# Seven-product 2x2 block groups in the gate and up projections, with the first weight sums on GpSimd

## What is computed

```python
x = x + jnp.concatenate([mix, mem_out], axis=-1) @ w_o[i]
gate, up = _split(rms_norm(x, norm_ffn[i]) @ w_gate_up[i], (D_FF, D_FF))
x = x + (jax.nn.silu(gate) * up) @ w_down[i]
```

## Time and profile before

| | |
|---|---|
| median of 3 runs | 2190.85 us (2190.31 to 2191.6) |
| the profiled execution, whole | 2190.48 us |
| its span in the profile | 2188.8 us |
| busy: TensorE, DVE, ACT, GpSimd | 99%, 59%, 47%, 3% of the span |
| bytes read from HBM | 411 MB, 189 GB/s over the span |

### The profile page before, as it was taken

The page is one execution under the profiler, slowest core; times in us unless marked ns, Lnnn a source line. Parts: engine busy times, 40 slices in busy tenths (PEclk is TensorE's granted clock), DMA queues, the critical chain, the costliest instruction groups (busy, mean ns, idle before and its releaser), DMA issues.

```text
span 2188.8 us, 29206 instructions
## 1 busy us (share of the span) xinstructions
PE 2175.4 (99%) x10172; PEld 1811.1 (83%) x10172; DVE 1293.3 (59%) x1555; ACT 1029.5 (47%) x1310; POOL 58.7 (3%) x99
## 2 busy tenths in 40 slices
PE   8999999999999999999999999999999999999999
PEld 7888888888888888888888888888888888888887
DVE  6767766555555555555566767675555555554443
ACT  7755654444444444444444445454444444443332
POOL 2101100000000000000100000000000000000000
PEclk9999999999999999999999999999999999999999
DMA  8765476766676666666555656577666766666664
GB/s 311 239 194 154 135 214 208 212 202 202 204 211 204 204 198 198 209 204 202 178 173 163 198 166 190 163 221 221 202 202 205 210 204 204 200 213 203 202 203 133
DMA packets 244562, 435.48 MB, mean 199 GB/s; under 512 B 23040, under 2 KB 43648, under 8 KB 244480
## 3 DMA queue, kind: packets, MB, share of 16 engines
q1 hardware_dynamic: 243392, 432.31, 64.8%
q10 hardware_dynamic: 1088, 2.10, 0.2%
HBM read 411.25 MB, written 2.10 MB: 189 GB/s over the span
## 4 chain that ended last, share of the span: by engine, by line
PE 99%; ACT 0%; DVE 0%; DMA 0%; issue 0%; DVEq 0%; SPq 0%; ACTq 0%
PE unit_bank L1629 95%; PE mix_bank L1652 1%; PE mix_bank L1782 1%; PE mix_bank L1717 0%; PE mix_bank L1679 0%; PE mix_bank L1726 0%; PE mix_bank L1768 0%; DVE w_lo L1005 0%; DMA source_T<-in_mem_T 0%; PE mix_bank L1690 0%; PE mix_bank L1701 0%; PE mix_bank L1813 0%; PE mix_bank L1811 0%; PE mix_bank L1804 0%; PE mix_bank L1794 0%; ACT p_a L675 0%
## 5 line engine op out<-in xcount | busy, mean ns | idle before, releaser
L1005 DVE TENSOR_TENSOR w_lo<-raw,w_hi 128x1024 fp32r<-128x1024 f32 x767 | 932.2, 1223 | 757.9 <-ACT w_hi L582 738.1
L582 ACT ACTIVATE w_hi<-raw 128x1024 fp32r<-128x1024 f32 x767 | 808.9, 1060 | 904.8 <-PE unit_bank L1629 875.4
L1629 PE MATMUL unit_bank<-w_hi,hT_hi 128*128 128x512 f32 (+1 forms) x1984 | 615.0, 391 | 0.0
L1629 PE MATMUL unit_bank<-w_hi,hT_lo 128*128 128x512 f32 (+1 forms) x1984 | 610.2, 389 | 0.0
L1629 PE MATMUL unit_bank<-w_lo,hT_hi 128*128 128x512 f32 (+1 forms) x1984 | 609.8, 389 | 0.0
L1629 PEld LDWEIGHTS unit_bank<-w_hi,hT_lo 128*128 128x128 f32 x1984 | 372.3, 188 | 76.5
L1629 PEld LDWEIGHTS unit_bank<-w_lo,hT_hi 128*128 128x128 f32 x1984 | 372.3, 188 | 76.5
L1629 PEld LDWEIGHTS unit_bank<-w_hi,hT_hi 128*128 128x128 f32 x1984 | 368.8, 188 | 72.8 <-DVE w_lo L1005 0.2
L1629 PE MATMUL unit_bank<-w_hi,gT_hi 128*128 128x512 f32 x704 | 217.0, 389 | 0.0
L1629 PE MATMUL unit_bank<-w_lo,gT_hi 128*128 128x512 f32 x704 | 216.9, 389 | 0.0
L1629 PE MATMUL unit_bank<-w_hi,gT_lo 128*128 128x512 f32 x704 | 216.8, 389 | 0.0
(11 more groups left out here) (232 smaller groups left out, 1028.3 us busy)
## 6 DMA issues: line engine op xcount, KB each, us to landing
raw<-in_w_gate_up SPq DMA_DIRECT2D x352, 512.0 KB, 4.3
raw<-in_w_down SPq DMA_DIRECT2D x176, 512.0 KB, 4.5
raw<-in_w_in_b SPq DMA_DIRECT2D x104, 512.0 KB, 4.0
raw<-in_w_o SPq DMA_DIRECT2D x64, 512.0 KB, 4.4
raw<-in_w_in_a SPq DMA_DIRECT2D x40, 512.0 KB, 4.1
moved<-turned SPq DMA_DIRECT2D x528, 32.0 KB, 3.1
raw<-in_w_mem_kv SPq DMA_DIRECT2D x31, 512.0 KB, 5.6
tanh_ff<-act_ff SPq DMA_DIRECT2D x112, 32.0 KB, 3.3
```

The costliest lines, as they stand in the source:

```text
L582: act.activation(w_hi[:, s, :, :], raw[:, s, :, :], ACT.Copy).then_inc(sems["hi_ready"], 1)
L1005: dve.tensor_tensor(w_lo[:, s, :, :], raw[:, s, :, :], w_hi[:, s, :, :].bitcast(F32), ALU.subtract).then_inc(sems["lo_ready"], 1)
L1629: ins = pe.matmul(unit_bank[2 * pair + tile][:, 0:cols], stationary[part][:, kt + j, tile * P:(tile + 1) * P], b[:, s, j, 0:cols], start=o ...
```

## The change

In the ten looped chunks of both layers, gate and up run side by side. The pieces of a chunk alternate: gate and up columns for the same 256 rows. Such a pair of pieces is a 2 x 2 block of weights (two row blocks; gate and up), and with the two token tiles and two feature blocks of `hT` it is a 2 x 2 by 2 x 2 block product. For two of the eight pairs of a chunk (`SEVEN = (2, 5)`) it is made from seven block products in place of eight, 21 matmuls of 512 columns in place of 24. That needs sums of activation blocks, made once for each layer (`seven_forms`, and the second token block in `hT` is overwritten by its difference from the first), and four sums of weight blocks for each group: two at once on GpSimd (`first_sums`, 1024 columns), two on DVE. Each sum is split into hi and lo like a weight. Four of the seven products go into the chunk's other four banks ("shared"); these are combined behind the group's last pieces (`shared_products`) and added to the chunk's own banks at its end (`own_products`), after which silu and the product with up follow in the next chunk. The first chunk of a layer has no groups.

The weights' side of a group, on ACT, GpSimd and DVE, and TensorE's order:

```diff
+                                pool.wait_ge(sems["hi_ready"], t.value("hi_ready"))
+                                pool.wait_ge(sems["piece_used"], t.value("split", RING))
+                                pool.tensor_tensor(sums[:, :, :], blocks[:, 1:3, :], blocks[:, 0:1, :].broadcast_to([P, 2, COLS]),
+                                                   ALU.add).then_inc(sems["sum_ready"], 1)
...
+            def split_seven():
...
+                act.wait_ge(sems["piece_used"], t.value("split", RING))
+                act.activation(four_blocks(w_hi, s)[:, 1:4, :], four_blocks(raw, s)[:, 1:4, :],
+                               ACT.Copy).then_inc(sems["hi_ready"], 2)
+                act.wait_ge(sems["sum_ready"], t.next("sum_ready"))
+                act.activation(sums_hi[:, :, :], sums[:, :, :], ACT.Copy).then_inc(sems["sum_hi_ready"], 1)
+                act.wait_ge(sems["sum_ready"], t.next("sum_ready"))
+                act.activation(w_hi[:, s, 0, :], w_sum[:, s, 0, :], ACT.Copy).then_inc(sems["sum_hi_ready"], 1)
+                act.wait_ge(sems["lo_ready"], t.value("split"))
+                act.activation(sum_all_hi[:, :], sum_all[:, :], ACT.Copy).then_inc(sems["sum_hi_ready"], 1)
...
+            def split_seven():
...
+                dve.wait_ge(sems["hi_ready"], t.next("hi_ready", 2))
...
+                dve.tensor_tensor(low[:, 1:4, :], blocks[:, 1:4, :], high[:, 1:4, :].bitcast(F32),
+                                  ALU.subtract).then_inc(sems["raw_lo_ready"], 1)
+                dve.wait_ge(sems["sum_ready"], t.next("sum_ready"))
+                dve.tensor_tensor(w_sum[:, s, 0, :], sums[:, 1, :], blocks[:, 1, :], ALU.add).then_inc(sems["sum_ready"], 1)
+                dve.wait_ge(sems["sum_ready"], t.next("sum_ready"))
+                dve.tensor_tensor(sum_all[:, :], w_sum[:, s, 0, :], blocks[:, 3, :], ALU.add).then_inc(sems["lo_ready"], 2)
+                dve.wait_ge(sems["sum_hi_ready"], t.next("sum_hi_ready"))
+                dve.tensor_tensor(sums_lo[:, :, :], sums[:, :, :], sums_hi[:, :, :].bitcast(F32),
+                                  ALU.subtract).then_inc(sems["sum_lo_ready"], 1)
+                dve.wait_ge(sems["sum_hi_ready"], t.next("sum_hi_ready"))
+                dve.tensor_tensor(w_lo[:, s, 0, :], w_sum[:, s, 0, :], w_hi[:, s, 0, :].bitcast(F32),
+                                  ALU.subtract).then_inc(sems["sum_lo_ready"], 1)
+                dve.wait_ge(sems["sum_hi_ready"], t.next("sum_hi_ready"))
+                dve.tensor_tensor(sum_all_lo[:, :], sum_all[:, :], sum_all_hi[:, :].bitcast(F32),
+                                  ALU.subtract).then_inc(sems["sum_lo_ready"], 1)
...
+                pe.wait_ge(sems["raw_lo_ready"], t.next("raw_lo_ready"))
+                product(own[1], x12, w_hi[:, s + 1, 1, :], w_lo[:, s + 1, 1, :], False, False)
+                product(own[0], form[2], w_hi[:, s, 1, :], w_lo[:, s, 1, :], False, False)
+                if first:
+                    pe.wait_ge(sems["shared_free"], t.next("shared_free"))
+                product(shared[0], x11, w_hi[:, s + 1, 0, :], w_lo[:, s + 1, 0, :], first, last)
+                pe.wait_ge(sems["sum_lo_ready"], t.next("sum_lo_ready"))
+                product(shared[1], form[0], sums_hi[:, 1, :], sums_lo[:, 1, :], first, last)
+                product(shared[2], x21_less_x11, sums_hi[:, 0, :], sums_lo[:, 0, :], first, last)
+                pe.wait_ge(sems["sum_lo_ready"], t.next("sum_lo_ready"))
+                product(shared[3], form[1], w_hi[:, s, 0, :], w_lo[:, s, 0, :], first, last)
+                pe.wait_ge(sems["sum_lo_ready"], t.next("sum_lo_ready"))
+                product(own[3], x22, sum_all_hi[:, :], sum_all_lo[:, :], False, False).then_inc(sems["piece_used"], 2)
```

`product` is three matmuls into one bank. The order within a chunk, for position i of 16 (DVE; ACT has the same with `gate_tanh` at 1, a copy of `shared[0]` at 12 and `moved_block` at 14), and SP's:

```diff
+                    for i in chunk_pieces():
                         if i == 1:
+                            gate_silu()
+                        if i == 5:
+                            times_up()
+                        if i == 13:
+                            shared_products(shared)
+                        if i == 14:
+                            moved_block(gT, j * 4, "gT_ready")
+                    own_products(own)
...
+                chunk_turns = moves({11: (0, 6), 12: (6, 12), 13: (12, 16)})
```

More of the change, by code:

```diff
@@ L63 @@
 LEVELS = 7
+QUAD_PIECES = 2
+CHUNK_PIECES = KT
+SEVEN = (2, 5)
+SEVEN_APART = 6
 MASKED = -1e38
@@ L1014, in pieces, with chunk_pieces @@
                         split()
+                    t.move("at")
+            def split_seven():
+                s = slot[0] % RING
+                slot[0] += 2
+                dve.wait_ge(sems["hi_ready"], t.next("hi_ready", 2))
+                t.move("split", 2)
+                dve.wait_ge(sems["piece_used"], t.value("split", RING))
+                blocks, low, high = (four_blocks(ring, s) for ring in (raw, w_lo, w_hi))
+                dve.tensor_tensor(low[:, 1:4, :], blocks[:, 1:4, :], high[:, 1:4, :].bitcast(F32),
[13 more added lines that the diff above has]
+                                  ALU.subtract).then_inc(sems["sum_lo_ready"], 1)
+            def chunk_pieces():
+                for i in range(CHUNK_PIECES):
+                    yield i
+                    ahead = (i + LEAD) % CHUNK_PIECES
+                    if ahead // 2 not in SEVEN:
+                        split()
+                    elif ahead % 2 == 0:
+                        split_seven()
                     t.move("at")
@@ L1472, in times_up @@
[L1472 to L1480, removed]
-                        if i == 1:
-                            moved_block(gT, (j - 1) * 4, "gT_ready")
-                    times_up()
+                        ins = dve.scalar_tensor_tensor(out=up_ff[:, s, :], in0=up_ff[:, s, :],
+                                                       scalar=half_rs2[:, s:s + 1], in1=tanh_ff[:, s, :], op0=ALU.mult,
+                                                       op1=ALU.mult)
@@ new lines, in chunk_products @@
+            def chunk_products(own, shared):
+                pe.wait_ge(sems["own_free"], t.next("own_free"))
+                for q in range(CHUNK_PIECES // 2):
+                    if q in SEVEN:
+                        seven_products(SEVEN.index(q), own, shared)
+                        continue
+                    for n in range(2):
+                        s = slot[0] % RING
+                        slot[0] += 1
+                        pe.wait_ge(sems["lo_ready"], t.next("lo_ready"))
+                        for j in range(2):
+                            for m, (part, b) in enumerate(((0, w_hi), (1, w_hi), (0, w_lo))):
+                                for tile in range(TILES):
+                                    ins = pe.matmul(own[2 * tile + n][:, :], hT[part][:, 2 * q + j, tile * P:(tile + 1) * P],
+                                                    b[:, s, j, :], start=q == 0 and j == 0 and m == 0,
+                                                    stop=q == CHUNK_PIECES // 2 - 1 and j == 1 and m == 2)
+                        ins.then_inc(sems["piece_used"], 1)
@@ L1901, in projection_ffn @@
                     pass
-                parts = [unit(hT, p, kts, opens=n == 0, closes=n == 2) for n, kts in enumerate(FIRST_KTS) for p in (pair, other)]
+                parts = [unit(hT, p, kts, opens=n == 0, closes=n == 2) for n, kts in enumerate(FIRST_KTS) for p in (2, 3)]
+                settled(0, 1, 2, 3)
                 for i in products(*parts):
```

217 lines of the change are left out of this document (176 added, 41 removed).

## The result

The changed kernel takes 2211.86 us (median of 4 runs, 2211.76 to 2213.44) beside 2190.9 before: a ratio of 1.0098, 95% interval 1.0083 to 1.0113. 1% slower; forecast were 2208 us and slower with a chance of 0.78. The profiled execution took 2211.83 us, its span 2210.0, 21.2 us over that of before.

A forecast was written before the change was run, and what follows sets the result against it. TensorE's matmul count was taken as the bound: 2190.5 - 27.2 us for matmuls removed + 40 x 1.12 us of waits for GpSimd's held-up sum = 2208 us, range 2190 to 2233.

The forecast's parts named there:

- What bounds, and what is saved: TensorE's matmul count bounds the kernel; 40 groups with 3 matmuls fewer each take 27.2 us off if it never waits.
- GpSimd held up by DVE's instruction: In each group, GpSimd's sum waits for DVE's whole three-block subtraction and ends at 3.35 + T us.
- Rival 1: GpSimd's sum is not held up by DVE's subtraction, so all of the saving stays: 2163.3 us; chance 0.13.
- T = 2.38 us: Time of GpSimd's 1024-column sum by itself: 2.38 us, the middle of 1.95 and 2.82.
- Rival 2: GpSimd's sum takes two steps a column, T near 1.95 us; the wait eats the saving: 2190 us; chance 0.07.
- The wait, 1.12 us: TensorE waits T - 1.26 = 1.12 us for `sums_lo` at each group's tenth matmul, against 0.68 saved: +17.6 us.
- the prediction's zero: The moment at which TensorE begins the second piece ahead of a group; the group's steps are timed from it.
- Rival 3: Five hand-overs on the chain at 0.08 us, not 0.04: +8 us, with T = 2.82 2233 us; chance 0.05.
- Rival 4: GpSimd goes first and DVE's subtraction waits; `w_sum` 0.1 us sooner, same time within 4 us; chance 0.03.
- DVE's, ACT's and SP's queues at no cost: In a chunk, the added DVE work, ACT's copies and SP's later loads delay nothing; DVE has 35.8 of 44.4 us.
- A chunk of 44.4 us: A looped chunk was forecast to take 44.4 us, with TensorE idle about 1.1 us in each group.

The follow-up runs named there:

- experiment 1: Changed kernel with DVE's subtraction of the three low parts made to wait until GpSimd's sum is done: 2218.71 us, ratio 1.0128.
- experiment 4: Changed kernel with `sum_all` moved behind `sums_lo` in DVE's queue, nothing else changed: 2236.57 us, ratio 1.0208.
- experiments 1 and 2: The second: changed kernel with DVE's subtraction of 1536 columns split into three instructions of 512: 2212.44 us, ratio 1.0099. The first: see experiment 1.
- experiment 3: Changed kernel with GpSimd's sum made twice in a row: 2380.33 us, ratio 1.0865; with only half the sum, 512 columns: 2177.83 us, ratio 0.9940.

## Why the prediction was right

- **What bounds, and what is saved.** Right. TensorE runs 120 matmuls fewer and is the bound wherever it doesn't wait; the kernel with DVE's sum first gets 20 of the 27.2 us.
- **GpSimd held up by DVE's instruction.** This step decided the sign, and it held. It rested on `head_ms` at 1.10 against 0.20 us, operations of eight columns with one input; experiment 1 shows it for 1024 columns and two inputs (3.9 against 2.40 us). GpSimd ended 2.25 us after DVE, where 0.06 + 2.38 - 0.20 = 2.24 was computed. Rival 1 is refuted.
- **T = 2.38 us.** Measured alone 2.40. It was the middle between two and three steps a column and not derived, so that the close hit is partly luck; the slope, 2.1 ns a column, is 2.5 of the one-input steps of the earlier trace rows. The estimate from "GPSIMD Engine Reference" of the Trainium skill, section 3.1 Elementwise, 2.25 to 2.35 us, was nearly as good: the trace agrees to within 0.05 to 0.15 us. Rival 2 (1.95) is refuted.
- **The wait, 1.12 us.** Measured 1.18, in the place named. The small difference is two larger ones that nearly cancel, which is luck. The chain up to the end of `sums_lo` was counted too short by 0.17 us: from the prediction's zero it ends at 8.49 us (mean of the forty groups) and not at 5.94 + 2.38 = 8.32. Of this, ACT's start is 0.08 (0.28 in place of 0.20), and the step from the start of `w_sum` to that of `sum_all` is another 0.08: 0.80 us (756.21 to 757.01), not the 0.72 that I took. `sum_all` waits there for `w_sum`, which DVE itself has just made. The last step, from DVE's end until TensorE goes on, was counted too long by 0.12 us: 0.28 was taken from TensorE's first matmuls, where a pair takes nearly 1 us, and in the loop it is 0.05 + 0.11 = 0.16. What remains, 0.06 x 40, is 2 us of the 4 by which the forecast was low. Rival 3's slow hand-over is seen at `sum_all` alone; DVE answers ACT and GpSimd in 0.03 to 0.06 us.
- **Rival 4**, the other order, gives 2218.7 us (experiment 1), 7 us over the changed kernel where "within 4 us" was said. The prediction says that `w_sum` comes 0.1 us sooner in that order. By its own numbers it is 0.1 later: the subtraction ends at 5.9, and the forecast's `w_sum` starts at 3.35 + 2.38 + 0.04 = 5.77. Measured, it starts 0.16 later (6.03 us after zero, 5.87 in the changed kernel), and 40 x 0.16 = 6.4 of the 7 us.
- **DVE's, ACT's and SP's queues at no cost.** Right as to this kernel: DVE is busy 34.8 us of a chunk (35.8 computed) and no plain piece is waited for. But they had less to spare than "nothing" suggests: experiment 4 shows that one instruction moved back by some 1.4 us in DVE's queue brings 29 us of new waits.
- **A chunk of 44.4 us:** measured 44.56.

## What to carry to other kernels

An engine at 3% is not free capacity if its operations and the busy one's exclude each other, as GpSimd's sum and DVE's two-input operations do here (experiments 1 and 2). The times of two such operations are added up, whichever queue they stand in, and the total goes on the path of whoever waits for both. Before moving work off a busy engine, look at whether that engine is idle at just that moment; here DVE waited 2.3 us for a sum that it makes in 1.2. And when an instruction is moved within a queue, list everything that its semaphores release: operands, the heads of other queues, and buffers for the next loads.

## What the hardware showed that I had not expected

TensorE's granted clock outlasts the waits of the changed kernel, 0.9 us idle each and 1.5 at the longest (it is 1.00 throughout), and not those of 3.3 us in experiment 3: matmuls of 512 columns then start 0.43 us apart in place of 0.23 for some 3 us, 1.9 us lost on top of each wait. And a matmul that had to wait costs 0.11 us more to the next start even at full clock (758.89 to 759.23, 0.34 in place of 0.23).
